# Norms' sums in a fp32 transformer kernel: where the low parts are made and where the products stand

## The reference

```python
for l in range(DEPTH):                              # 2 layers
    h = rmsnorm(x, g_mix)
    p = h @ w_in                                    # c_q 384 | c_kv 256 | rope 32 | a 512 | gt 512
    q = rmsnorm(p_cq, g_q) @ w_uq ;  kv = rmsnorm(p_ckv, g_kv) @ w_ukv
    y_attn = attention(q, k, v)                     # 8 heads
    u = dwconv31(a * sigmoid(gt))
    u = silu(layernorm(u, g_conv_ln, b_conv_ln))
    x = x + concat([y_attn, u]) @ w_o
    z = dwconv3(rmsnorm(x, g_ffn) @ w_up)           # 2 x 2816
    x = x + (silu(zg) * zv) @ w_down
x = rmsnorm(x, g_final)
# second block: compressed, selected and windowed attention, out norms, w_out, a second FFN
```

## Time and profile before

| What | Value |
|---|---|
| median of three runs | 1923.36 us |
| the profiled execution | 1924.04 us, span 1922.2 us |
| TensorE (PE) | busy 1834.1 us, 95% of the span |
| VectorE (DVE) | 1341.0 us, 70% |
| ScalarE (ACT) | 970.0 us, 50% |
| GpSimd (POOL) | 191.7 us, 10% |
| mean granted TensorE clock | 0.982 of full speed |

### The profile page before, as it was taken

One profiled execution on the slowest core, in us unless ns is written; L12 is line 12 of the kernel. 1 busy time (PEld: TensorE's weight loads), 2 busy tenths in 40 slices (PEclk: granted clock), 3 DMA queues, 4 the chain that ended last, 5 costly groups with the idle time before them and its releaser, 6 DMA issues.

```text
span 1922.2 us, 27068 instructions
## 1 busy us (share of the span) xinstructions
PE 1834.1 (95%) x8975; PEld 1459.0 (76%) x8975; DVE 1341.0 (70%) x1909; ACT 970.0 (50%) x1548; POOL 191.7 (10%) x135
## 2 busy tenths in 40 slices
PE   6899999999999889999999999997998999999998
PEld 5675688888888776678888888887565678888887
DVE  6889777777655789967777755595676477777543
ACT  5458764444433448855444433574655554444322
POOL 0200120000133100020000033200012300000010
PEclk9999999999999999999999999999999999999999
DMA  5230133333233311033333233434000223332332
GB/s 171 58 84 1 55 88 99 98 97 92 80 97 100 104 39 56 1 100 98 98 98 94 78 96 97 115 84 143 1 1 1 88 66 98 96 91 86 91 97 74
DMA packets 285095, 154.46 MB, mean 80 GB/s; under 512 B 16949, under 2 KB 283095, under 8 KB 285015
## 3 DMA queue, kind: packets, MB, share of 16 engines
q1 hardware_dynamic: 284596, 153.26, 27.5%
q10 hardware_dynamic: 419, 0.17, 0.0%
HBM read 151.31 MB, written 2.10 MB: 80 GB/s over the span
## 4 chain that ended last, share of the span: by engine, by line
PE 77%; DVE 12%; issue 6%; ACT 4%; DMA 0%; DVEq 0%; POOL 0%; SPq 0%; ACTq 0%; POOLq 0%
PE bank L536 23%; PE bank L537 23%; PE bank L538 23%; DVE cacc L1633 3%; PE bank L897 1%; DVE w_lo L1496 1%; PE bank L937 1%; PE bank L916 1%; DVE nmax L1699 1%; ACT w_hi L1092 1%; DVE pr L1940 1%; PE bank L683 1%; DVE nmax L1924 1%; DMA x_in<-in_x 0%; DVE tz L1507 0%
## 5 line engine op out<-in xcount | busy, mean ns | idle before, releaser
L1092 ACT ACTIVATE w_hi<-raw 128x1024 fp32r<-128x1024 f32 (+3 forms) x345 | 337.0, 985 | 549.5 <-PE bank L538 545.2
L1496 DVE TENSOR_TENSOR w_lo<-raw,w_hi 128x1024 fp32r<-128x1024 f32 (+3 forms) x345 | 406.9, 1186 | 280.7 <-ACT w_hi L1092 279.1
L536 PE MATMUL bank<-h_hi,w_hi 128*128 128x512 f32 x1448 | 571.8, 395 | 5.7 <-DVE w_lo L1496 5.3
L537 PE MATMUL bank<-h_lo,w_hi 128*128 128x512 f32 x1448 | 567.6, 392 | 0.0
L538 PE MATMUL bank<-h_hi,w_lo 128*128 128x512 f32 x1448 | 567.0, 392 | 0.0
L536 PEld LDWEIGHTS bank<-h_hi,w_hi 128*128 128x128 f32 x1448 | 274.6, 190 | 67.8 <-issue 6.4
L537 PEld LDWEIGHTS bank<-h_lo,w_hi 128*128 128x128 f32 x1448 | 274.3, 189 | 58.5 <-issue 1.9
L538 PEld LDWEIGHTS bank<-h_hi,w_lo 128*128 128x128 f32 x1448 | 274.4, 189 | 57.9
L536 PE MATMUL bank<-a_hi,w_hi 128*128 128x512 f32 x528 | 206.1, 390 | 0.0
L538 PE MATMUL bank<-a_hi,w_lo 128*128 128x512 f32 x528 | 205.5, 389 | 0.0
L537 PE MATMUL bank<-a_lo,w_hi 128*128 128x512 f32 x528 | 205.4, 389 | 0.0
(11 more groups left out here) (313 smaller groups left out, 2218.2 us busy)
## 6 DMA issues: line engine op xcount, KB each, us to landing
raw<-in_w_up SPq DMA_DIRECT2D x132, 512.0 KB, 3.7
raw<-in_w_in SPq DMA_DIRECT2D x39, 512.0 KB, 3.9
raw<-in_w_down SPq DMA_DIRECT2D x48, 384.0 KB, 3.1
raw<-in_w_down SPq DMA_DIRECT2D x48, 320.0 KB, 2.9
raw<-in_w_o SPq DMA_DIRECT2D x16, 512.0 KB, 3.5
raw<-in_cmp_w SPq DMA_DIRECT2D x8, 512.0 KB, 3.9
raw<-in_w_out SPq DMA_DIRECT2D x8, 512.0 KB, 4.4
raw<-in_w_uq SPq DMA_DIRECT2D x8, 288.0 KB, 3.0
```

Source lines behind the costliest of these rows:

```text
L536: mm(o, wh, mh, start=start, stop=False)
L537: mm(o, wh, ml, start=False, stop=False)
L1092: last = A_(dst(w_hi), src(raw), ACT.Copy)
L1496: last = v.tensor_tensor(dst(w_lo), src(raw), dst(w_hi).bitcast(f32), ALU.subtract)
```

## The change

Nothing is added to or removed from the arithmetic. Low parts, high parts, products and weight splits of the sums stand at other places in the lists of TensorE, ScalarE and VectorE.

- SUM_IN's products stand behind 21 matmuls of slab 1 instead of 12.
- SUM_CQ's low part is made between two halves of the taps of iteration 6 instead of at the head of iteration 7, its products stand behind 12 matmuls of slab 8 instead of ahead of that slab. SUM_CKV's low part is made directly behind the low parts of c_q in iteration 8, its high part on ScalarE ahead of the last high part of c_q, its products stand behind 21 matmuls of slab 10 instead of ahead of it.
- The last attended chunk's low part (`attended_low`) stands behind the low parts of SUM_MEAN and SUM_LAST; the products of both stand behind 12 matmuls of the out-projection.
- SUM_VAR's low part stands ahead of the split of S_O+3, its products 12 matmuls earlier; ScalarE's split of S_O+4 stands behind the second high part of `uq`, not ahead of the root, and VectorE's likewise.
- SUM_FFN's products stand behind 9 matmuls of the up-projection's second slab instead of ahead of it. SUM_NSA's stand 6 matmuls later.

```diff
--- before.py
+++ after.py
@@ -588,6 +588,8 @@
                                n == 0, n == KD - 1)
+                    if between:
+                        between(n)
@@ -627,15 +629,15 @@
                                    k == 0, k == KD - 1)
-                        if i == 1 and k == KD // 2 - 1:
+                        if i == 1 and k == KD - 2:
                             sum_parts(L, SUM_IN, s_in, 0)
+                        if i == I_CQ + 1 and k == KD // 2 - 1:
+                            pe.wait_ge(rstd_done.sem, rstd_done.at(L, 1))
+                            sum_parts(L, SUM_CQ, s_in, 1)
+                        if i == I_CKV + 1 and k == KD - 2:
+                            pe.wait_ge(rstd_done.sem, rstd_done.at(L, 2))
+                            sum_parts(L, SUM_CKV, s_in, 0)
                     last.then_inc(slab_used.sem, 1)
-                    if i == I_CQ:
-                        pe.wait_ge(rstd_done.sem, rstd_done.at(L, 1))
-                        sum_parts(L, SUM_CQ, s_in, 1)
-                    if i == I_CKV:
-                        pe.wait_ge(rstd_done.sem, rstd_done.at(L, 2))
-                        sum_parts(L, SUM_CKV, s_in, 0)
@@ -744,13 +746,14 @@
                 pe.wait_ge(y_lo.sem, y_lo.at(L, KC - 1))
-                for m in range(2):
-                    wo(m, 0, 0, KC - 1)
+                wo(0, 0, 0, KC - 1)
+                wo(1, 0, 0, 1)
...
                 sum_parts(L, SUM_MEAN, s_at, 1, stop=False)
+                sum_parts(L, SUM_LAST, s_at, 0, start=False)
+                wo(1, 0, 1, KC - 1)
...
                 wo(0, 0, KC - 1, KC)
-                sum_parts(L, SUM_LAST, s_at, 0, start=False)
@@ -758,7 +761,8 @@
                         last.then_inc(slab_used.sem, 1)
-                sum_parts(L, SUM_VAR, s_at, 1)
+                    if m == 4:
+                        sum_parts(L, SUM_VAR, s_at, 1)
@@ -771,10 +775,14 @@
                     last.then_inc(o_even.sem if i % 2 == 0 else slab_used.sem, 1)
+                def sum_ffn(n):
+                    if n == 2:
+                        pe.wait_ge(rstd_done.sem, rstd_done.at(L, 4))
+                        sum_parts(L, SUM_FFN, s_at, 0)
+
                 up_slab(g, L, 0, 0, S_UP, O_ORDER, KQ + KKV)
-                pe.wait_ge(rstd_done.sem, rstd_done.at(L, 4))
-                sum_parts(L, SUM_FFN, s_at, 0)
-                for s in range(1, 4):
+                up_slab(g, L, 0, 1, S_UP, O_ORDER, None, sum_ffn)
+                for s in range(2, 4):
@@ -970,13 +978,14 @@
                     pe.wait_ge(rstd_done.sem, rstd_done.at(N, 4))
-                last = out_part(m, 0, 0, PAIRS)
-                if m % 2 == 1:
-                    last.then_inc(slab_used.sem, 1)
-                if m == 2:
+                if m == 3:
+                    out_part(m, 0, 0, 2)
...
                     sum_parts(N, SUM_NSA, s_nsa, 0)
+                last = out_part(m, 0, 2 if m == 3 else 0, PAIRS)
+                if m % 2 == 1:
+                    last.then_inc(slab_used.sem, 1)
@@ -1172,12 +1181,6 @@
                         A_(zr[:, 1, :], zr[:, 1, :], ACT.Exp, bias=lneb[:, :]).then_inc(ve_done.sem, 1)
-                    if i == I_CQ:
-                        act.wait_ge(ssq_done.sem, ssq_done.at(L, Q_CQ))
-                        sum_high(s_in, 1, ssq[:, :])
-                    if i == I_CKV:
-                        act.wait_ge(ssq_done.sem, ssq_done.at(L, Q_CKV))
-                        sum_high(s_in, 0, ssq[:, :])
@@ -1189,12 +1192,18 @@
                         A_(craw[:, j, :], bank[i % 7][:, :], ACT.Copy).then_inc(c_copy.sem, 1)
+                    if i == I_CQ - 1:
+                        act.wait_ge(ssq_done.sem, ssq_done.at(L, Q_CQ))
+                        sum_high(s_in, 1, ssq[:, :])
...
                     if i == I_CQ + 1:
-                        for c in range(KQ):
+                        for c in range(KQ - 1):
                             op_high(L, c, c_hi[:, c, :], c)
+                        act.wait_ge(ssq_done.sem, ssq_done.at(L, Q_CKV))
+                        sum_high(s_in, 0, ssq[:, :])
+                        op_high(L, KQ - 1, c_hi[:, KQ - 1, :], KQ - 1)
@@ -1287,7 +1296,6 @@
                 sum_high(s_at, 1, ssq[:, :])
-                split(L, g, S_O + 2 + SPL)
@@ -1296,6 +1304,8 @@
                     A_(uq[:, c, 0, :], tz[:, c, :], ACT.Copy).then_inc(u_hi.sem, 1)
+                    if c == 1:
+                        split(L, g, S_O + 2 + SPL)
@@ -1637,10 +1647,6 @@
                         sum_low(L, SUM_IN, s_in, 0, ssq[:, :])
-                    if i == I_CQ:
-                        sum_low(L, SUM_CQ, s_in, 1, ssq[:, :])
-                    if i == I_CKV:
-                        sum_low(L, SUM_CKV, s_in, 0, ssq[:, :])
@@ -1661,6 +1667,7 @@
                         op_gen(L, 0, KQ, craw, lambda c: col(C_GQ + c), lambda c: 1, c_hi, c_lo)
+                        sum_low(L, SUM_CKV, s_in, 0, ssq[:, :])
@@ -1668,6 +1675,10 @@
                         conv(3, 3 * TAPS)
+                    elif i == I_CQ - 1:
+                        conv(3, 2 * TAPS - TAPS_ALONE)
+                        sum_low(L, SUM_CQ, s_in, 1, ssq[:, :])
+                        conv(3, 2 * TAPS - TAPS_ALONE)
@@ -1699,10 +1710,12 @@
                         inverse(s - 1)
-                    if s >= NT + 4 and (s - 4) % NT == 0:
-                        c = (s - 4) // NT - 1
-                        dve.wait_ge(y_hi.sem, y_hi.at(L, c + 1))
-                        v.tensor_tensor(yq[:, c, 1, :], O_B[c % 2][:, :], yq[:, c, 0, :].bitcast(f32), ALU.subtract).then_inc(y_lo.sem, 1)
+                    if NT + 4 <= s < SU + 4 and (s - 4) % NT == 0:
+                        attended_low((s - 4) // NT - 1)
+
+                def attended_low(c):
+                    dve.wait_ge(y_hi.sem, y_hi.at(L, c + 1))
+                    v.tensor_tensor(yq[:, c, 1, :], O_B[c % 2][:, :], yq[:, c, 0, :].bitcast(f32), ALU.subtract).then_inc(y_lo.sem, 1)
@@ -1714,7 +1727,7 @@
                 inverse(2)
-                for s in range(3, SU + 5):
+                for s in range(3, SU + 4):
@@ -1724,13 +1737,13 @@
                 sum_low(L, SUM_LAST, s_at, 0, cacc[:, KC - 1, :])
+                attended_low(KC - 1)
...
                     v.scalar_tensor_tensor(cacc[:, c, :], STAT[:, :], -1.0 / CCH, cacc[:, c, :], ALU.mult, ALU.add).then_inc(cen_done.sem, 1)
-                for i in range(2):
-                    split(g, S_O + i + SPL)
+                split(g, S_O + SPL)
                 sum_low(L, SUM_VAR, s_at, 1, ssq[:, :])
-                split(g, S_O + 2 + SPL)
+                split(g, S_O + 1 + SPL)
@@ -1739,6 +1752,8 @@
                     v.tensor_tensor(uq[:, c, 1, :], tz[:, c, :], uq[:, c, 0, :].bitcast(f32), ALU.subtract).then_inc(u_lo.sem, 1)
+                    if c == 1:
+                        split(g, S_O + 2 + SPL)
...
```

## The result

The changed kernel takes 1907.36 us (median of 4 runs, 1907.14 to 1908.6) against 1923.98 us for the kernel before in the same comparison: ratio 0.9915, 95% interval 0.9901 to 0.9929. The forecast was 1907.7, its range 1901.5 to 1915. The profiled execution took 1908.6 us.

The account below looks back on a forecast made before the run. VectorE's list was taken as the bound, its idle time (8.77 and 8.25 us) as what can return. Terms -14.9 - 1.25 - 1.6 + 2.8 - 0.7 = -15.65 gave 1908.4 from 1924.04, median 1907.7 us, range 1901.5 to 1915.

Parts of the forecast that it names:

- part 1: Moves for SUM_CQ and SUM_CKV, slab 8 to second query slab: 7.7 and 7.2 us faster by layer, -14.9 together.
- Rival A: TensorE sets the pace: the whole 14.0 and 13.5 us of the two layers come back, 1895.1 us; chance 0.08.
- The new waits: TensorE waits for weight splits (`w_lo`) at slabs 10, 11, 13 and both query slabs: 1.6, 1.4, 1.5, 0.2, 1.1 us.
- The collision: VectorE's taps against GpSimd's two operations for SUM_CKV: one added per layer, 1.05 us; bounds none and two.
- Part 3: Convolution's norm, SUM_VAR earlier but split S_O+4 needed first: -0.8 us a layer, -1.6 together; bounds 0 and 1.9.
- Part 4: SUM_FFN's later products delay the up-projection's slab 2: 1.4 us slower a layer, +2.8 together; bounds 0 and 1.6.
- B: The covers hold: no extra collision (-2.1) and the SUM_FFN chain hidden (-2.8), 1902.8 us; chance 0.10.
- C: New gaps lower the clock at the second query slab and behind SUM_FFN, 1.7 us each: +6.8, 1914.5 us; chance 0.10.
- D: Slower: gaps keep TensorE at 1.2 GHz from slab 10 to the first query slab, 1951 us; chance 0.02.
- E: Waits for sums return whole as waits for splits, VectorE's idle time stays, small parts remain: 1922.6 us; chance 0.04.

Follow-up runs that it names:

- e3: Kernel before with only the products of SUM_CQ and SUM_CKV moved into slabs 8 and 10, low and high parts left in place: 1907.16 us.
- e5: Changed kernel with 21 convolution taps a layer on 128 columns instead of 512, so work is left out: 1897.48 us.
- e6: Changed kernel with GpSimd's two operations for SUM_CKV on 8 columns instead of 512, so work is left out: 1905.28 us.
- e9: Kernel of e8 with four convolution taps moved from iteration 7 into iterations 1 and 2: 1899.08 us.
- e10: Kernel before with four convolution taps moved from iteration 7 into iterations 1 and 2: 1922.90 us, ratio 1.0003.
- e7: Changed kernel with SUM_FFN's products put back ahead of slab 1 of the up-projection: 1905.25 us.
- e8: Changed kernel with the split of the up-projection's slab 2 ahead of the norm's root on ScalarE, and moved ahead on VectorE alike: 1906.07 us.
- e4: Kernel before with 18 and 17 useless matmuls added ahead of the products of SUM_CQ and SUM_CKV: 1917.05 us.
- e2: Kernel before with only the low and high parts of SUM_CQ and SUM_CKV moved, products left ahead of slabs 8 and 10: 1912.28 us.

## Why the prediction was right

- **The decisive step** was to read VectorE's idle time as the upper bound of what part 1 can bring. Forecast 7.7 and 7.2, measured 8.0 and 7.5. e3 shows that waits for sums can come back without cost, e5, e6 and e9 that the stretch shrinks by what is taken out of VectorE's list, and e10 that the same taps bring next to nothing where idle time is left. Rival A had 14.0 and 13.5; e5 shows that it lacked the shorter list.
- **The new waits** were forecast at slabs 10, 11, 13 and the two query slabs with 1.6, 1.4, 1.5, 0.2 and 1.1 us. They are 1.33, 0.93, 1.29, none listed and 0.69: right in place, 0.2 to 0.5 too long. The forecast list had split 15 end at 113.8; it ended at 113.2, and 0.4 of that is that slab 7 ended that much earlier.
- **The collision** was the term least known. Two collisions are there, and e6 puts them at 1.09 us each. The kernel before had one in the same stretch, at 85.93 (its row stands in the last section). The value taken (one added, 1.05) holds; the bound of two added does not occur.
- **Part 3** was under-sized a little, -0.8 against -1.0 in each layer. The split S_O+4 comes first and is waited for as said (`w_lo`, 0.40 us instead of 0.7), as TensorE's timeline after shows:

```profile
231.39 0.50 PE L536 MATMUL bank<-uq,w_hi 128*128 128x512 f32 x1 [0.40 <-DVE w_lo L1506]
```

- **Part 4** had the right sign, a loss, although the edit removes a wait there: +1.4 against +1.5, and e7 and e8 confirm cause and size. So B's second half falls; its first, no added collision, falls by e6.
- **C and D**: behind the waits of 0.7 to 1.7 us the clock stays at 1.00 in every stretch read. D has nothing for it. C's 6.8 us did not come either. Low clock elsewhere cost 1.1 us in sum, but at places that the change does not touch, and with gains beside the losses, so not by C's mechanism.
- **The total** agrees better than its parts (1907.7 against 1907.36): part 1 brought 0.6 us more, part 3 0.4 more, and the clock elsewhere took 1.1 back in the profiled execution. That the total agrees to 0.3 us is luck.
- **E** falls: VectorE's idle time did not stay.

What stays open is why low-clock stretches come in the attention or the second block of one trace and not of another. No experiment here sets them.

## What to carry to other kernels

Where a feeding engine's list spans the same stretch and stays as long as it is, waits on the busiest engine are worth at most the feeder's idle time there (here 8.0 of 8.8 us came back, not 14.0). So read the feeder's list over the stretch before adding up the waits. When a wait disappears, look for the in-order engine whose list was late anyway; its work then pays in full, and moving it into earlier idle time (e9) brings what removing more waits can't. A result that nobody needs soon may stand far behind on the engine that makes it, but if a load or a split is queued behind its consumer, that queue decides how late (SUM_FFN).

## What the runs showed of the hardware

- Matmuls of no use during two waits of 4.6 and 4.3 us gave back 3.8 to 4.3 us a layer (e4): at 1.2 GHz TensorE delivers its slabs late, and engines that wait for them lose the time. Behind the four waits of 0.7 to 1.3 us in each stretch of the changed kernel the clock stayed at 1.00. In layer 0 of e2 it stayed so behind a wait of 2.64 us and was low (0.60 over 4 us) behind one of 3.41 us. In layer 1 of e2 it was the other way: low behind a wait of the same 2.64 us, and full behind the second, of 2.73 us. So the length of the wait alone did not tell. TensorE's rows of e2 in layer 1, and the clock behind each:

```profile
663.65 0.50 PE L547 MATMUL bank<-s_in,ones_r 128*128 128x512 f32 x1 [2.64 <-DVE s_in L1517]
679.63 0.50 PE L547 MATMUL bank<-s_in,ones_r 128*128 128x512 f32 x1 [2.73 <-DVE s_in L1517]
664.00:668.00 4.00, 4.00 (x13) 3.21 (x12) 4.00 (x5) 2.13 (x4) 1.50 (x1) 0.64 0.10 27
679.00:683.00 4.00, 3.37 (x15) 2.80 (x16) 4.00 (x6) 2.71 (x4) 0.00 (x0) 1.00 0.00 0
```

- GpSimd and VectorE: the two taps of the changed kernel that meet an add take 1.09 us more each. Not every meeting costs VectorE time. GpSimd's own operations got shorter in the changed kernel, the first 1.35 us where it had taken 3.00. GpSimd's timeline after:

```profile
75.35 1.35 POOL L2014 TENSOR_TENSOR ssq<-csq,zr 128x512 f32<-128x512 f32 x1 [7.86 <-ACT zr L1200]
77.86 1.30 POOL L2019 TENSOR_TENSOR ssq<-ssq,csq 128x512 f32<-128x512 f32 x1 [1.16 <-ACT csq L1193]
```

  VectorE beside the two adds of the kernel before (78.04 and 85.39). Two taps keep their pace; the pair of products at 85.93 takes 2.45 us where it takes 1.41 in the changed kernel:

```profile
78.50 1.40 DVE L1633 SCALAR_TENSOR_TENSOR cacc<-u_pad,lc,cacc 128x512 f32<-128x512 f32 x2
85.93 2.45 DVE L1507 SCALAR_TENSOR_TENSOR tz<-craw,lc,rstd 128x512 f32<-128x512 f32 x2
```

  The Trainium skill (SBUF — State Buffer, Who interferes with whom) says that issue order decides who blocks. The recorded starts here do not bear it out: the add at 78.04 began ahead of the two taps at 78.50, yet the taps kept their pace and the add took 3.00 us; in the changed kernel the add at 77.86 was short and held a tap that had begun at 77.84. Either the recorded start is not the moment that counts, or more than the order decides; no run here separates the two.
